# Expert weights loaded in 8 KB runs, with the inner channels reordered as the weights are split on ScalarE and VectorE

## The chip, the cores and the metric

The kernel runs on one core of a Trainium2 chip. The metric is device time in microseconds (us), from the start of the program to its end. Engines are PE (TensorE: matmuls; PEld its weight loads), DVE (VectorE), ACT (ScalarE), POOL (GpSimd) and SP (SyncE, which here only issues DMAs).

## The reference

One layer over 2048 latent tokens of width 1024 with a context prefix of 256: a mixing sub-layer (retention and Mamba-2 heads) and then a mixture of gated-MLP experts. The change is in the second. Each token picks one of 4 groups and two of its 8 experts, and each of the 32 experts works on its tokens in blocks of 128:

```python
def expert_block(args):
    tok, e = args
    xb = h_pad[tok]
    hid = jax.nn.silu(xb @ w_gate[e]) * (xb @ w_up[e])
    return hid @ w_down[e]
```

Per expert, `w_gate` and `w_up` are 1024 x 512 and `w_down` is 512 x 1024, all fp32: 2 MB each. The router's logits are `h @ w_rg` and `h @ w_re`, from the same normed rows `h`.

## The kernel before

The program has five stages: `front`, `states`, `mixing`, then `residual` and `experts` in one program, and `combine`. Every product is made of three: a value is split into a high part (rounded to fp32r) and a low part (the rest), and high x high, high x low and low x high are summed in PSUM.

**residual** goes through 16 tiles of 128 tokens. Per tile it makes the output projection, `x1`, and from it the normed rows `h2`: L2257 scales and L2259 adds, both on DVE, over 128 x 1024. PE transposes `h2` (L2101) in eight chunks of 128 columns, multiplies by the router's weights (L2058), and ACT sends `h2` to `second_norm` in HBM, from which the experts gather their rows. Between L2257 of a tile and its transposes PE works on the products of another tile (L2049). DVE then does the routing (L2186 to L2241). In turns 3 to 8 SP issues the loads of expert 0, and in the last turn ACT makes the high part of its first third (L2138), ahead of its copy L2160.

**experts** holds one expert's weights whole in `raw` (`e_w_whole`), and their parts in `wh` (`e_w_high`) and `wl` (`e_w_low`), each as three thirds of 4096 elements per partition. Third 0 is gate and up for the inner channels 0 to 255, third 1 those for 256 to 511, third 2 is the down weights. SP loads each third as two sixths of 1 MB (`load_sixth`): row `k * 128 + p` of gate or up goes to partition p, 256 elements (1 KB) at a time, and rows of down whole, 4 KB. A third of the next expert is loaded when DVE has made the low part of the one in `raw` (`wls`).

A block of 128 tokens is one turn of `body` on each engine. On PE:

- 24 matmuls for the first 256 inner channels, gate and up side by side in one PSUM bank (L2513 high x high, L2514 high x low, L2517 low x high), which need third 0; then 24 for the other 256, which need third 1;
- transposes of the first half of the hidden values (`turn_h`, L2501) and of the next block's rows (`turn_x`, L2494);
- 24 matmuls for down (L2522), 8 of them ahead of the transposes of the second half of the hidden values.

ACT: Silu of each half of the gate (L2578), copies of the transposed hidden values (L2585) and rows (L2566), half of the output (L2593). DVE: Silu(gate) x up x router's weight (`hid`, L2628), the low parts of the transposed values (L2633, L2612), the other half of the output (L2640).

In the last block of an expert (`following` is the next expert) ACT also makes the next expert's high parts (L2573, two instructions of 128 x 2048 per third) and DVE its low parts (L2619, the same): third 0 between the two halves of Silu and of `hid`, third 1 after the transposed hidden values, third 2 after the output. There are 48 blocks for 32 experts in these inputs, so 31 blocks have such a follower's weights to make; below they are called **splitting blocks**. An expert of several blocks goes through `body` without this work first; one of a single block has only a splitting block, so splitting blocks also come one behind the other.

## Time and profile before

| | |
|---|---|
| median of 3 runs | 2333.85 us (2333.26 to 2334.17) |
| profiled execution | 2337.66 us, its span 2336.0 us |
| PE busy | 2177.8 us, 93% |
| DVE busy | 1400.3 us, 60% |
| ACT busy | 1055.3 us, 45% |
| POOL busy | 643.1 us, 28% |
| DMA | 518.11 MB, mean 222 GB/s |

The shares are means over the five stages. The stage of the experts, which the change concerns most, is from 1386.8 us of the span (first matmul) to 2277 us (end of the last).

### The profile page before, as it was taken

What the parts mean: (1) busy time and instruction counts of PE and PEld (TensorE: products, weight loads), DVE (VectorE), ACT (ScalarE), POOL (GpSimd) and SP (SyncE); (2) the same over time, 40 slices, a digit from 0 to 9 for tenths busy, and PEclk for the clock granted to TensorE, in tenths of its full rate; (3) what the DMA queues carried; (4) which work ended last, traced back from release to release, by engine and by line L of the source; (5) the groups of instructions that cost most, each with busy time, mean ns of one, the idle gap of its engine ahead of it and who ended that gap; (6) DMA issues with size and microseconds to landing.
All of it is one profiled execution on the core that took longest, in us unless ns stands there. A gap on an engine that the chain in (4) does not pass through costs nothing. (4 is left out here: it accounts for less than half of the span.)

```text
span 2336.0 us, 35426 instructions
## 1 busy us (share of the span) xinstructions
PE 2177.8 (93%) x11618; PEld 1836.8 (79%) x11619; DVE 1400.3 (60%) x2033; ACT 1055.3 (45%) x1518; POOL 643.1 (28%) x648
## 2 busy tenths in 40 slices
PE   8999999999999679998999979999999999999990
PEld 5888888899999568887788858778788888887770
DVE  6322222377555578887566665765767675647776
ACT  4422332243223026665333234755666665547763
POOL 0000000000000558887222232221333333323333
PEclk9999999999999889999999989999999999999995
DMA  8632333546551987765554335998988887868997
GB/s 308 237 108 109 127 142 139 187 158 214 175 175 54 333 331 240 233 220 203 160 214 150 118 124 168 344 285 256 338 263 268 270 276 244 252 174 278 350 347 302
DMA packets 297436, 518.11 MB, mean 222 GB/s; under 512 B 33492, under 2 KB 206108, under 8 KB 292584
## 3 DMA queue, kind: packets, MB, share of 16 engines
q1 hardware_dynamic: 271000, 439.52, 55.1%
q0 software_dynamic: 17136, 43.92, 8.4%
q10 hardware_dynamic: 9216, 33.56, 3.5%
q8 instruction: 51, 0.84, 0.2%
q14 instruction: 33, 0.27, 0.0%
HBM read 397.28 MB, written 128.57 MB: 225 GB/s over the span
## 5 line engine op out<-in xcount | busy, mean ns | idle before, releaser
L2619 DVE TENSOR_TENSOR e_w_low<-e_w_whole,e_w_high 128x2048 fp32r<-128x2048 f32 x192 | 431.1, 2287 | 90.6 <-ACT e_w_high L2573 87.1
L2573 ACT ACTIVATE e_w_high<-e_w_whole 128x2048 fp32r<-128x2048 f32 x190 | 353.9, 1914 | 30.2 <-DMA e_w_whole<-in_moe_w_down_dram 18.5
L2513 PE MATMUL r_py<-e_w_high,e_xT 128*128 128x512 f32 x768 | 298.9, 389 | 1.2 <-ACT e_xT L2566 1.2
L2514 PE MATMUL r_py<-e_w_low,e_xT 128*128 128x512 f32 x768 | 298.8, 389 | 0.0
L897 PE MATMUL proj_acc<-w_high,hT_high 128*128 128x512 f32 x672 | 263.9, 393 | 0.3 <-DVE hT_low L1010 0.3
L897 PE MATMUL proj_acc<-w_low,hT_high 128*128 128x512 f32 x672 | 262.0, 390 | 0.0
L897 PE MATMUL proj_acc<-w_high,hT_low 128*128 128x512 f32 x672 | 261.7, 389 | 0.0
L2522 PE MATMUL r_py<-e_w_high,e_hT 128*128 128x512 f32 x768 | 226.7, 407 | 18.0 <-ACT e_hT L2585 17.9
L2517 PE MATMUL r_py<-e_w_high,e_xT 128*128 128x512 f32 x768 | 189.9, 389 | 0.0
L2522 PEld LDWEIGHTS r_py<-e_w_high,e_hT 128*128 128x128 f32 x768 | 138.6, 191 | 45.8 <-ACT e_hT L2585 20.6
L2513 PEld LDWEIGHTS r_py<-e_w_high,e_xT 128*128 128x128 f32 x768 | 144.2, 188 | 31.3 <-issue 1.4
L2517 PEld LDWEIGHTS r_py<-e_w_high,e_xT 128*128 128x128 f32 x768 | 144.2, 188 | 29.9
L2514 PEld LDWEIGHTS r_py<-e_w_low,e_xT 128*128 128x128 f32 x768 | 144.2, 188 | 29.9
L887 PE MATMUL proj_acc<-hT_high,w_high 128*128 128x256 f32 x576 | 164.4, 285 | 0.0
L887 PE MATMUL proj_acc<-hT_low,w_high 128*128 128x256 f32 x576 | 164.1, 285 | 0.0
L887 PE MATMUL proj_acc<-hT_high,w_low 128*128 128x256 f32 x576 | 164.0, 285 | 0.0
L1230 DVE SCALAR_TENSOR_TENSOR conv_out<-ch,cw,conv_out 128x258 f32<-128x258 f32 x288 | 119.4, 480 | 72.3 <-ACT conv_out L805 72.2
L897 PEld LDWEIGHTS proj_acc<-w_high,hT_high 128*128 128x128 f32 x672 | 126.5, 188 | 29.5 <-issue 3.5
L897 PEld LDWEIGHTS proj_acc<-w_high,hT_low 128*128 128x128 f32 x672 | 126.3, 188 | 26.5
L897 PEld LDWEIGHTS proj_acc<-w_low,hT_high 128*128 128x128 f32 x672 | 126.4, 188 | 24.9
L2049 PE MATMUL r_py<-r_w_high,r_yT 128*128 128x512 f32 x512 | 142.1, 394 | 0.0
L2423 POOL COPY e_rows_held<-e_rows_held 128x6 int32<-128x6 int32 x48 | 32.2, 672 | 360.6 <-issue 253.1
(311 smaller groups left out, 4196.2 us busy)
## 6 DMA issues: line engine op xcount, KB each, us to landing
e_w_whole<-in_moe_w_gate_dram SPq DMA_DIRECT2D x64, 1024.0 KB
e_w_whole<-in_moe_w_up_dram SPq DMA_DIRECT2D x64, 1024.0 KB
e_w_whole<-in_moe_w_down_dram SPq DMA_DIRECT2D x64, 1024.0 KB
by_token<-tok SPq DMA_DIRECT2D x32, 512.0 KB, 3.0
w_in_raw<-in_w_mod_dram SPq DMA_DIRECT2D x32, 512.0 KB, 4.4
m_tok<-by_token SPq DMA_DIRECT2D x16, 768.0 KB, 5.5
s_kv<-by_token SPq DMA_DIRECT2D x20, 512.0 KB, 5.9
modulated_high<-hT_high SPq DMA_DIRECT2D x9, 1024.0 KB, 3.9
```

What stands on the lines that cost most here:

```text
L887: m = nc.tensor.matmul(bank[:, b * 2 * P:(b + 1) * 2 * P], a[:, PLACE[c], k, w], h[:, s, k], start=(k == 0 and n == 0), stop=(k == KD - 1 ...
L897: m = nc.tensor.matmul(bank, h[:, s, k, span], (wh if high_ else wl)[:, PLACE[c], k], start=(k == 0 and n == 0), stop=(k == KD - 1 and n = ...
L1230: V.scalar_tensor_tensor(out=v[:, c], in0=chb[:, c, k:k + OUT], scalar=cw[:, k, c:c + 1], in1=v[:, c], op0=ALU.mult, op1=ALU.add).then_inc ...
L2049: m = nc.tensor.matmul(py[:, s, n], yT[:, s, part, k], with_[:, k, n * 512:(n + 1) * 512], start=(k == 0 and part == 0 and with_ is wh), s ...
L2423: nc.gpsimd.tensor_copy(held[:, 0:2], held[:, 1:3]).then_inc(held_on.sem, 1)
L2513: nc.tensor.matmul(pG[:, half], xT[:, 0, k], wh[:, half, w], start=(k == 0), stop=False)
L2514: nc.tensor.matmul(pG[:, half], xT[:, 0, k], wl[:, half, w], start=False, stop=False)
L2517: m = nc.tensor.matmul(pG[:, half], xT[:, 1, k], wh[:, half, k * 512:(k + 1) * 512], start=False, stop=(k == KD - 1))
L2522: m = nc.tensor.matmul(pY[:, n], hT[:, part, k], with_[:, 2, c0:c0 + 512], start=first, stop=last)
L2573: nc.scalar.activation(wh[:, third, part], raw[:, third, part], ACT.Copy).then_inc(whs.sem, 1)
L2619: nc.vector.tensor_tensor(wl[:, third, part], raw[:, third, part], wh[:, third, part].bitcast(F32), ALU.subtract).then_inc(wls.sem, 1)
```

## The change

1. **Loads.** Partition p now takes rows `8p` to `8p + 7` of gate and up. Third 0 holds the first four of these rows with all 512 inner channels of gate and of up, third 1 the other four: one run of 8 KB per partition and sixth. Of down it takes rows `4p` to `4p + 3`, two per sixth, again one run of 8 KB.
2. **Order of the model's channels.** `h2` is written by DVE so that chunk k of its transposes holds channels `8p + k` (`by_chunks`, in L2257 and L2259), and the router's weights are loaded to match.
3. **Order of the inner channels.** Chunk c of the hidden values must hold channels `4q + c`, so gate and up are put in that order as they are split: for thirds 0 and 1 ACT reads `raw` with steps of four elements (16 bytes) and writes runs of 128, and DVE does the same (`sixth_of`). For down both read as before. Gate and up of a chunk lie side by side, and Silu and `hid` read them in runs of 128.
4. **Order of the work.** Third 0 now has half of the rows of all products, so PE makes 24 matmuls with it for both halves of the inner channels, says so (`rows_done`), then 12 with third 1 that end the first half and 12 that end the second. In a splitting block ACT and DVE make the first sixth of the next expert after `rows_done`, ahead of the first Silu and `hid`, and the second sixth behind them.

```diff
@@ residual @@
-                nc.vector.scalar_tensor_tensor(out=h2[:, 1 - s], in0=x1[:, 1 - s], scalar=ss[:, 3:4], in1=g["mod"][:, 2], op0=ALU.mult, op1=ALU.mult).then_inc(h2m.sem, 1)
+                nc.vector.scalar_tensor_tensor(out=by_chunks(h2[:, 1 - s]), in0=by_rows(x1[:, 1 - s]), scalar=ss[:, 3:4], in1=by_rows(g["mod"][:, 2]), op0=ALU.mult, op1=ALU.mult).then_inc(h2m.sem, 1)
...
-                nc.vector.tensor_tensor(h2[:, 1 - s], h2[:, 1 - s], g["mod"][:, 1], ALU.add).then_inc(h2s.sem, 1)
+                nc.vector.tensor_tensor(by_chunks(h2[:, 1 - s]), by_chunks(h2[:, 1 - s]), by_rows(g["mod"][:, 1]), ALU.add).then_inc(h2s.sem, 1)
@@ load_sixth @@
-        to = raw[:, third].rearrange("p (k n f) -> p k n f", k=KD, n=2)[:, :, n]
-        eng.dma_start(to, io[src][0, bass.ds(e, 1), :, third * 256:(third + 1) * 256].rearrange("o (k p) f -> p (o k) f", p=P)).then_inc(landed, 16)
+        rows = KD // 2
+        to = raw[:, third, n * THIRD // 2:(n + 1) * THIRD // 2].rearrange("p (k f) -> p k f", k=rows)
+        eng.dma_start(to, io[src][0, bass.ds(e, 1)].rearrange("o (p k) f -> p (o k) f", k=KD)[:, third * rows:(third + 1) * rows]).then_inc(landed, 16)
...
+def sixth_of(buf, third, n, whole):
+    if third == 2:
+        return buf[:, third, n * THIRD // 2:(n + 1) * THIRD // 2]
+    if whole:
+        return buf[:, third, n * THIRD // 2:(n + 1) * THIRD // 2].rearrange("p (k q c) -> p k c q", q=P, c=DE // P)
+    return buf[:, third].rearrange("p (k c n q) -> p k c n q", c=DE // P, n=2, q=P)[:, :, :, n]
@@ experts, tensor @@
+            pe.wait_ge(xTs.sem, xTs.at(b))
+            pe.wait_ge(wls.sem, wls.at(expert_of[0], 2))
             for half in range(2):
                 pe.wait_ge(hids.sem, hids.at(b - 1, half + 1))
...
+                gate_up(half, 0, 0)
+            pe.wait_ge(xTl.sem, xTl.at(b))
+            for half in range(2):
+                m = gate_up(half, 1, 0)
+            m.then_inc(rows_done.sem, 1)
+            pe.wait_ge(wls.sem, wls.at(expert_of[0], 4))
+            for half in range(2):
+                gate_up(half, 0, 1)
+                gate_up(half, 1, 1).then_inc(prodG.sem, 1)
@@ experts, scalar @@
+        def high_sixth(third, n):
+            nc.scalar.activation(sixth_of(wh, third, n, False), sixth_of(raw, third, n, True), ACT.Copy).then_inc(whs.sem, 1)
...
         def body(b, row, following):
+            if following is not None:
+                act.wait_ge(w_in.sem(0), w_in.at(following))
+                act.wait_ge(rows_done.sem, rows_done.at(b))
+                high_sixth(0, 0)
@@ experts, vector @@
+        def low_sixth(e, third, n):
+            dve.wait_ge(whs.sem, whs.at(e, 2 * third + n + 1))
+            nc.vector.tensor_tensor(sixth_of(wl, third, n, False), sixth_of(raw, third, n, True), sixth_of(wh, third, n, False).bitcast(F32), ALU.subtract).then_inc(wls.sem, 1)
```

How this moves instructions, on ACT, from the start of a splitting block to the copy of the last transposed hidden values. Before (L2578 is Silu into `e_sg`, L2573 makes a high part, L2585 and L2566 are the copies):

```order
L2578 ACT_TABLE_LOAD
L2578 ACTIVATE e_sg<-r_py 128x256
L2570 ISA
L2573 ACTIVATE e_w_high<-e_w_whole 128x2048 x2
L2577 REGISTER_ALU
L2578 ACTIVATE e_sg<-r_py 128x256
...
L2585 ACTIVATE e_hT<-r_pl 128x256
...
L2566 ACTIVATE e_xT<-r_pT 128x1024
L2585 ACTIVATE e_hT<-r_pr 128x256
```

Now the same place of the changed kernel (its L2613 is Silu, L2598 makes a high part, L2619 and L2595 are the copies):

```order
L2598 ACT_TABLE_LOAD
L2598 ACTIVATE e_w_high<-e_w_whole 128x16x128
L2612 ISA
L2613 ACT_TABLE_LOAD
L2613 ACTIVATE e_sg<-r_py 128x256
L2598 ACTIVATE e_w_high<-e_w_whole 128x16x128
L2612 REGISTER_ALU
L2613 ACTIVATE e_sg<-r_py 128x256
L2619 ACTIVATE e_hT<-r_pl 128x256
...
L2595 ACTIVATE e_xT<-r_pT 128x1024
L2619 ACTIVATE e_hT<-r_pr 128x256
```

One conversion stands ahead of the first Silu and one behind it, and there are two loads of an activation table where there was one.

On DVE, the same block from its first `hid` on, before (L2628 makes `hid`, L2619 a low part of the weights):

```order
L2628 SCALAR_TENSOR_TENSOR e_hid<-e_sg,e_rows_held,r_py 128x256
L2618 ISA
L2619 TENSOR_TENSOR e_w_low<-e_w_whole,e_w_high 128x2048
L2618 REGISTER_ALU
L2619 TENSOR_TENSOR e_w_low<-e_w_whole,e_w_high 128x2048
...
L2628 SCALAR_TENSOR_TENSOR e_hid<-e_sg,e_rows_held,r_py 128x256
L2633 TENSOR_TENSOR e_hT<-r_pl,e_hT 128x256
```

and now (L2650 makes a low part, L2666 makes `hid`):

```order
L2650 TENSOR_TENSOR e_w_low<-e_w_whole,e_w_high 128x16x128
...
L2666 SCALAR_TENSOR_TENSOR e_hid<-e_sg,e_rows_held,r_py 128x256
L2649 REGISTER_ALU
L2650 TENSOR_TENSOR e_w_low<-e_w_whole,e_w_high 128x16x128
...
L2666 SCALAR_TENSOR_TENSOR e_hid<-e_sg,e_rows_held,r_py 128x256
L2671 TENSOR_TENSOR e_hT<-r_pl,e_hT 128x256
```

The first low part has moved ahead of the first `hid`; the number of instructions is the same.

## Rows read from the trace of the kernel before

**Rows 1.** Windows: us, busy time (instructions) of each engine, PEclk, DMA share, GB/s.
```profile
1387.00:2277.00 890.00, 862.58 (x4032) 710.94 (x4031) 583.60 (x476) 541.50 (x520) 272.49 (x241) 0.99 0.88 275
1110.00:1340.00 230.00, 224.95 (x1233) 194.07 (x1234) 148.00 (x364) 73.47 (x134) 63.65 (x104) 0.98 0.47 163
2290.00:2336.00 46.00, 0.00 (x0) 0.00 (x0) 37.65 (x32) 18.39 (x32) 17.68 (x16) 0.50 0.92 365
```
**Rows 2.** Timeline of PE, first gate-up matmul of six blocks: start, us, instruction.
```profile
1386.79 0.49 PE L2513 MATMUL r_py<-e_w_high,e_xT 128*128 128x512 f32 x1 [1.19 <-ACT e_xT L2566]
...
1505.91 0.39 PE L2513 MATMUL r_py<-e_w_high,e_xT 128*128 128x512 f32 x1
...
1506.36 0.39 PE L2513 MATMUL r_py<-e_w_high,e_xT 128*128 128x512 f32 x1
...
1526.81 0.39 PE L2513 MATMUL r_py<-e_w_high,e_xT 128*128 128x512 f32 x1
...
1544.52 0.39 PE L2513 MATMUL r_py<-e_w_high,e_xT 128*128 128x512 f32 x1
...
1562.23 0.39 PE L2513 MATMUL r_py<-e_w_high,e_xT 128*128 128x512 f32 x1
...
2259.08 0.39 PE L2513 MATMUL r_py<-e_w_high,e_xT 128*128 128x512 f32 x1
```
**Rows 3.** Groups of instructions, 1340 to 2290: count, busy us, mean ns, idle before.
```profile
L2619 DVE TENSOR_TENSOR e_w_low<-e_w_whole,e_w_high 128x2048 fp32r<-128x2048 f32 x192 | 431.1, 2287 | 90.6 <-ACT e_w_high L2573 87.1 <-issue 3.4
L2573 ACT ACTIVATE e_w_high<-e_w_whole 128x2048 fp32r<-128x2048 f32 x190 | 353.9, 1914 | 30.2 <-DMA e_w_whole<-in_moe_w_down_dram 18.5 <-DMA e_w_whole<-in_moe_w_up_dram 11.7
L2578 ACT ACT_TABLE_LOAD x47 | 60.3, 1283 | 1.1 <-issue 0.3
L2612 DVE TENSOR_TENSOR e_xT<-r_pT,e_xT 128x1024 fp32r<-128x1024 f32 x49 | 59.8, 1220 | 21.6 <-ACT e_xT L2566 21.4
L2566 ACT ACTIVATE e_xT<-r_pT 128x1024 fp32r<-128x1024 f32 x49 | 50.3, 1028 | 25.7 <-PE r_pT L2494 25.7
L2628 DVE SCALAR_TENSOR_TENSOR e_hid<-e_sg,e_rows_held,r_py 128x256 f32<-128x256 f32 x96 | 45.6, 476 | 125.4 <-ACT e_sg L2578 106.9 <-POOL e_rows_held L2423 18.4
L2578 ACT ACTIVATE e_sg<-r_py 128x256 f32<-128x256 f32 x96 | 36.7, 382 | 138.3 <-PE r_py L2517 137.8
L2640 DVE COPY e_y<-r_py 128x512 f32<-128x512 f32 x48 | 32.9, 686 | 65.6 <-DMA rows_summed<-e_y,e_rows_held 42.3 <-PE r_py L2522 23.3
L2593 ACT ACTIVATE e_y<-r_py 128x512 f32<-128x512 f32 x48 | 28.6, 595 | 91.9 <-DMA rows_summed<-e_y,e_rows_held 64.7 <-PE r_py L2522 27.2
L2633 DVE TENSOR_TENSOR e_hT<-r_pr,e_hT 128x256 fp32r<-128x256 f32 x48 | 20.1, 420 | 6.9 <-ACT e_hT L2585 6.9
L2585 ACT ACTIVATE e_hT<-r_pr 128x256 fp32r<-128x256 f32 x48 | 18.5, 386 | 66.0 <-PE r_pr L2501 64.9 <-issue 1.0
```
**Rows 4.** Timeline of DVE in the splitting block that began at 1544.52.
```profile
1556.80 0.48 DVE L2628 SCALAR_TENSOR_TENSOR e_hid<-e_sg,e_rows_held,r_py 128x256 f32<-128x256 f32 x1
```
**Rows 5.** Groups of instructions on DVE, whole span, small and strided ones among them.
```profile
L2206 DVE TENSOR_REDUCE o_s<-o_w 128x8 f32<-128x32 f32 x16 | 3.4, 211 | 0.5
L2235 DVE TENSOR_REDUCE o_sl<-o_wr 128x2 f32<-128x64 f32 x16 | 3.5, 220 | 0.5
L2199 DVE TENSOR_SCALAR o_og<-o_expert_number,o_group_first 128x4 f32<-128x4 f32 x16 | 3.7, 229 | 0.6
L2200 DVE TENSOR_SCALAR o_d<-o_l,o_m 128x4 f32<-128x4 f32 x16 | 3.7, 229 | 0.6
L1812 DVE TENSOR_TENSOR m_t<-m_t 128x512 f32<-128x512 f32 x16 | 20.5, 1279 | 0.0
```
**Rows 6.** DMA queues, 1387 to 2277: packets, MB, share of 16 engines.
```profile
q1 hardware_dynamic: 147718, 202.62, 66.5%
```
**Rows 7.** Timeline of a turn of the residual stage: second step of `h2`, and PE's transposes.
```profile
1300.32 1.23 DVE L2259 TENSOR_TENSOR r_h<-r_h,mod 128x1024 f32<-128x1024 f32 x1
1303.31 1.03 PE L2101 MATMUL r_pT<-ident,r_h 128*128 128x128 f32 x8
```

More of the change, by code:

```diff
@@ L2347, in experts @@
     prodG = kit.counter("e_gate_up", 2, credit=2)
+    rows_done = kit.counter("e_first_rows_used")
     sgs = kit.counter("e_silu", 2, credit=2)
@@ L2504, in body, with gate_up @@
         def body(b, row, following, e=None):
+            def gate_up(half, part, rows):
+                for k in range(4):
+                    w = slice((2 * k + half) * 512, (2 * k + half + 1) * 512)
+                    if part == 0:
+                        nc.tensor.matmul(py[:, 0, half], xT[:, 0, 4 * rows + k], wh[:, rows, w], start=(rows == 0 and k == 0), stop=False)
+                        nc.tensor.matmul(py[:, 0, half], xT[:, 0, 4 * rows + k], wl[:, rows, w], start=False, stop=False)
+                    else:
+                        m = nc.tensor.matmul(py[:, 0, half], xT[:, 1, 4 * rows + k], wh[:, rows, w], start=False, stop=(rows == 1 and k == 3))
+                        if k == 3:
+                            return m
+            pe.wait_ge(xTs.sem, xTs.at(b))
+            pe.wait_ge(wls.sem, wls.at(expert_of[0], 2))
             for half in range(2):
                 pe.wait_ge(hids.sem, hids.at(b - 1, half + 1))
[L2508 to L2518 removed]
+                gate_up(half, 0, 0)
[7 more added lines that the diff above has]
+                gate_up(half, 1, 1).then_inc(prodG.sem, 1)
             def down(k, part, with_, first=False, last=False):
@@ L2571, in high @@
             for n in range(2):
-                part = slice(n * HALF, (n + 1) * HALF)
-                nc.scalar.activation(wh[:, third, part], raw[:, third, part], ACT.Copy).then_inc(whs.sem, 1)
+                high_sixth(third, n)
         def body(b, row, following):
+            if following is not None:
+                act.wait_ge(w_in.sem(0), w_in.at(following))
+                act.wait_ge(rows_done.sem, rows_done.at(b))
+                high_sixth(0, 0)
             for half in range(2):
                 act.wait_ge(prodG.sem, prodG.at(b, half + 1))
-                nc.scalar.activation(sg[:, half], pG[:, half, 0], ACT.Silu).then_inc(sgs.sem, 1)
+                nc.scalar.activation(sg[:, half].rearrange("p (c q) -> p c q", c=2), pG[:, half, :, 0], ACT.Silu).then_inc(sgs.sem, 1)
                 if following is not None and half == 0:
-                    high(following, 0)
+                    high_sixth(0, 1)
             for half in range(2):
@@ L2627, in body @@
                     dve.wait_ge(held_on.sem, held_on.at(b + 2))
-                nc.vector.scalar_tensor_tensor(out=hid[:, half * 256:(half + 1) * 256], in0=sg[:, half], scalar=held[:, 1, 2:3].bitcast(F32), in1=pG[:, half, 1], op0=ALU.mult, op1=ALU.mult).then_inc(hids.sem, 1)
+                nc.vector.scalar_tensor_tensor(out=hid[:, half * 256:(half + 1) * 256].rearrange("p (c q) -> p c q", c=2), in0=sg[:, half].rearrange("p (c q) -> p c q", c=2), scalar=held[:, 1, 2:3].bitcast(F32), in1=pG[:, half, :, 1], op0=ALU.mult, op1=ALU.mult).then_inc(hids.sem, 1)
                 if following is not None and half == 0:
-                    low(following, 0)
+                    low_sixth(following, 0, 1)
             for half in range(2):
```

33 lines of the change are left out of this document (13 added, 20 removed).

## Prediction

> **What bounds the kernel now.** I read the windows by stage first. In the expert stage, 890 us of the span, PE is busy for 862.6 us at a granted clock of 0.99, the upper of its levels (2.4 GHz); DVE is busy for 583.6 and ACT for 541.5, and the DMA engines for 0.88 of the time [rows 1]. So PE sets the end, but nothing is far from full. Then PE's timeline: a block of 128 tokens takes 17.7 us where nothing holds it (1544.52 to 1562.23), with a matmul of 512 columns every 0.226 us, and 20.9 us in others (1505.91 to 1526.81) [rows 2]. From the first block's start to the last one's, 47 blocks, are 872.3 us, 40 more than 47 x 17.71. Counting all starts, ten blocks of 19.9 to 21.7 us hold 31 us of that; they are all splitting blocks that stand behind another splitting block. There are 17 such blocks (I call them **chained**), and 14 splitting blocks stand behind one that does not split. The chained ones take 19.6 us on average. The other excess is mostly the first block's.
>
> What stretches the ten is DMA: ACT sits idle for 30.2 us ahead of its conversions because weights have not landed [rows 3], and what it then makes late delays Silu and PE. That is what longer runs can mend. But the groups also show how little room DVE has. A splitting block holds six low parts of 2.287 us, two `hid` of 0.476, two small low parts of 0.42, one of 1.220 and a copy of 0.686: 17.4 us, in 17.7. ACT has six of 1.914, one table load of 1.283, two Silu of 0.382, two copies of 0.386, one of 1.028 and one of 0.595: 15.9 us [rows 3]. Whatever makes DVE's conversions dearer becomes the period of the chained blocks at once.
>
> **The price of a 16-byte step.** This decides the case. Four of the six conversions now read `raw` so, on both engines. No large instruction here does it; one small one does. L2206 reduces 32 elements that lie 32 bytes apart and takes 211 ns. L2235, the same operation on neighbours, takes 220 ns for 64 [rows 5]. An element costs DVE (2287 - 1220) / 1024 = 1.04 ns [rows 3], so 32 neighbours would take 187. The steps add 24 ns, 0.76 ns an element, and 1.56 us on 2048: a low part of thirds 0 and 1 takes 3.84 us instead of 2.29. Lower bound: no extra, as L2199, with four stepped elements, takes the 229 ns of L2200 with four neighbours (3 ns would be due). Upper bound: 2.5 ns an element, the slowest DVE row (L1812, 512 elements in 1279 ns) [rows 5], 5.1 us. I take the row with the most stepped elements.
>
> The Trainium skill, page "Vector Engine (DVE) Microarchitecture Reference", section "Measured stream behaviour on trn2", says that a port runs at full rate only on runs of at least two adjacent 4-byte words, and gives 1.73 against 1.05 ns per column if one source hops each element. From that page the estimate would be 3.7 us; L2206 agrees.
>
> ACT has no stepped row. Lower bound nothing, 1.91 us; upper bound DVE's whole 3.84. I take the same share of an element as on DVE: 0.76 / 1.04 of ACT's 0.865 ns ((1914 - 1028) / 1024 [rows 3]) is 0.63, so 1.29 us more, 3.20.
>
> **A splitting block behind a block that does not split (14).** From its first matmul: PE has used third 0 after 24 matmuls, at 5.4 us. ACT makes the first sixth until 8.6, loads a table (the second such load in the block, by the order) until 9.9, Silu until 10.3, second sixth until 13.5, second Silu 13.9. DVE makes its sixth from 8.6 to 12.5, `hid` until 12.9, the second sixth from 13.5 to 17.3, second `hid` until 17.8. PE, done with gate and up at 10.9, waits for the first `hid`, works on and waits for the second. That one ends now at 12.8 us (1557.28 [rows 4]), with 5.0 to the next block; 4.0 of these are PE's own work (16 matmuls and two transposes). So the block ends at about 22.0 instead of 17.7: 14 x 4.3 = 60 us.
>
> **The block behind it (14).** ACT's high parts of third 1 are ready at about 21.6 and 24.8, DVE's low parts at 25.4 and 29.3. PE wants them at 22.0 + 5.4 = 27.4 and waits 1.9. DVE's copy and third 2 end at 34.6, 12.6 into this block, and the two `hid` at 13.6, where PE wants the first at 12.8: 0.8. 14 x 2.7 = 38 us.
>
> **A chained splitting block (17).** DVE's own work is 17.4 + 4 x 1.56 = 23.6 us, ACT's 15.9 + 1.3 + 4 x 1.29 = 22.4. Neither fills its time: a low part starts only after its high part, and the first sixth only after PE's 24 matmuls. DVE's idle time before L2619 is now 90.6 us, 2.9 per expert [rows 3]; I leave 1.9. Period 25.5 instead of 19.6: 17 x 5.9 = 100 us. The waits for DMA, some 33 us, are in the 19.6 and so given back here. With this period transfers are hidden: q1 takes 66.5% of 890 us for 202.6 MB, 2.92 us per MB [rows 6], 18 us for an expert's 6.3 MB even at today's price.
>
> **Residual stage.** `h2` is written with 512-byte steps: L2257 costs 0.8 us more for 1024 elements, L2259, which also reads so, 0.8 to 1.6. It ends now 1.8 us ahead of PE's transposes (1301.55 to 1303.31) [rows 7], so a tile adds 0 to 0.6 us; the last tile's, on the way to the routing, adds 1.6 to 2.4 in full. ACT's two early conversions (L2138) stand before the last tile's copy and add up to 2.6, partly at the same time. Together 4 us, between 2 and 14. The router's weight loads and the loads' issues cost nothing: SP is not waited for.
>
> **Sum.** 60 + 38 + 100 + 4 = 202 us. The profiled execution took 2337.7 us (its span 2336.0), 3.8 above the median of the runs: 2337.7 + 202 - 3.8 = 2536 us.
>
> **Rivals.**
> - *The steps are free* (the side of faster). For it: L2199. The Trainium skill speaks for it too: "SBUF — State Buffer", section "Door 1: The DMA port swizzle", has in its note on cachelines that one can "stride for free" over 4 fp32, though it also wants two hits in a 16-byte line, which this step never has; by that rule the time is this rival's. Against it: L2206, where the excess is eight times what L2199 could hide. Then DMA decides: with 4 KB runs the combine stage has 365 GB/s at a DMA share of 0.92 [rows 1], 2.5 us per MB against 2.9. Gate and up, 4.2 MB an expert, save 1.7 us or more of the 3.1 that a long block loses, so some 18 of 33 us come back. Against that stand the table load and the second `hid`, which ends 0.9 us later (13.7 in place of 12.8); 0.3 of that reaches PE in 31 blocks, 9 us. 2337.7 - 9 - 3.8 = 2325 us. It decides if a step costs DVE less than about 0.2 ns, where 17.4 us of work begin to exceed what the block leaves.
> - *Only DVE pays.* ACT has its own access and no row speaks. Then the first low part starts at 7.4 and the second `hid` ends at 16.0: 14 x 2.4 = 34; the block behind 14 x 1.6 = 22; chained blocks at DVE's 23.6 and 0.9 of waits, 17 x 4.9 = 83. With 4: 143 us, 2477. If a step costs DVE half, about 2410.
> - *Steps cost much more*, as L1812's 2.5 ns would have it on DVE with ACT at 3.84. DVE then has 28.7 us in a chained block and a period near 30.7: 17 x 11.1 = 189, the pairs 14 x 10 = 140, residual 14: about 2675. Against: POOL works beside L1812, and L2206 shows half of its excess per element.
> - *The change doesn't do what it says*: excluded by the order, which shows the conversions as 128x16x128.
>
> **Chances.** Both pay as forecast 0.54, only DVE 0.22, free 0.15, much more 0.09. The point is the likeliest, 2536. The range runs from 2400 (only DVE, at half price) to 2640 (ACT at DVE's price gives 50 to 60 us more, and the cheap end of the last case); it leaves out the free case and the far end of the dear one. About 0.2% (5 us) is what a measurement can tell from no change. Faster by more 0.13, within 0.03, slower 0.84.
>
> **What would show it.** In the profile of the changed kernel: L2650 with the form 128x16x128 near 3.8 us on DVE and L2598 near 3.2 on ACT, while 128x2048 stay at 2.29 and 1.91; two table loads per splitting block; PE waiting for `hid` (transposes L2501's successors) and for low parts of third 1; starts of chained blocks 25 to 26 us apart; ACT no longer idle for weights; q1's time per MB lower although nobody gains by it; the DMA share falling with the longer stage. L2257's successor near 2.0 us. I am wrong if the stepped form takes 2.3 us on DVE, and wrong on the path if it takes 3.8 and blocks stay at 18 to 20 us.

## The result and the profile after

The changed kernel takes **2627.33 us** (median of 4 runs, 2624.16 to 2630.29) against 2334.01 us (4 runs, 2333.26 to 2338.47) of the kernel before, run beside it: ratio 1.1243, 95% interval 1.1223 to 1.1263. It is 293 us slower; the forecast was 202 slower. The profiled execution has a span of 2624.5 us.

The windows by stage, changed kernel (us, busy time and instructions of PE, PEld, DVE, ACT, POOL, then the granted clock, DMA share, GB/s):

```profile
1398.00:2570.00 1172.00, 966.63 (x4032) 769.04 (x4032) 779.26 (x477) 823.34 (x553) 368.53 (x242) 0.91 0.63 209
1110.00:1340.00 230.00, 225.52 (x1234) 193.80 (x1235) 170.31 (x365) 73.62 (x134) 71.10 (x104) 0.98 0.47 163
2577.00:2624.00 47.00, 0.00 (x0) 0.00 (x0) 37.65 (x32) 18.39 (x32) 17.55 (x16) 0.50 0.90 358
```

Against [rows 1]: the expert stage, 890 us before, is 1172 long; the combine stage is as it was, and in the residual window PE's work is as it was, DVE is busier by 22 us and POOL by 7. In the expert stage DVE and ACT are busy for 196 and 282 us more. The DMA share falls from 0.88 to 0.63. The granted clock of TensorE falls from 0.99 to 0.91.

The costliest groups in the expert stage, changed kernel (line, engine, operation, out<-in, shapes, count | busy us, mean ns | idle before and what ended it):

```profile
L2650 DVE TENSOR_TENSOR e_w_low<-e_w_whole,e_w_high 128x2048 fp32r<-128x2048 f32 x190 | 628.7, 3333 | 253.0 <-ACT e_w_high L2598 245.5 <-issue 7.4
L2598 ACT ACTIVATE e_w_high<-e_w_whole 128x2048 fp32r<-128x2048 f32 x186 | 594.5, 3234 | 42.0 <-PE r_py L2530 41.8
L2527 PE MATMUL r_py<-e_w_high,e_xT 128*128 128x512 f32 x768 | 320.9, 418 | 87.6 <-DVE e_w_low L2650 86.3 <-ACT e_xT L2595 1.3
...
L2551 PE MATMUL r_py<-e_w_high,e_hT 128*128 128x512 f32 x768 | 245.4, 433 | 3.5 <-ACT e_hT L2619 3.3
```

The first two answer to L2619 and L2573 of [rows 3]. L2527 is one of PE's matmuls for gate and up; the same of the kernel before, from its profile page:

```profile
L2513 PE MATMUL r_py<-e_w_high,e_xT 128*128 128x512 f32 x768 | 298.9, 389 | 1.2 <-ACT e_xT L2566 1.2
```

One mean covers two kinds: a third of the conversions (down's) have no steps. With 2290 and 1916 ns for these (e3 below shows DVE's alone; ACT's 1916 is the mean of e1, which has no steps), the profile page's means over all 192 and 190 (3340 and 3227 ns) give (192 x 3340 - 64 x 2290) / 128 = 3865 ns for a stepped one on DVE and (190 x 3227 - 64 x 1916) / 126 = 3893 on ACT. ACT no longer sits idle for weights ahead of its conversions: nearly all of the idle time there is for PE (L2530).

Who waits, changed kernel, 1390 to 2570 us (engine, line, waited for: us in total, times, longest):

```profile
DVE e_w_low L2650 <- ACT e_w_high L2598: 245.5, 92, 8.5
...
PE r_pl L2519 <- DVE e_hid L2666: 91.3, 32, 5.7
PE r_py L2527 <- DVE e_w_low L2650: 86.3, 31, 2.9
...
ACT e_y L2627 <- DMA rows_summed<-e_y,e_rows_held: 24.7, 5, 5.6
```

PE waits 32 times for the first `hid` and 31 times for a low part of third 1; there are 31 splitting blocks. DVE in turn waits for ACT.

One chained splitting block. PE's timeline of the changed kernel has its start and the next (start, us, instruction), 27.7 us apart:

```profile
2489.22 0.39 PE L2527 MATMUL r_py<-e_w_high,e_xT 128*128 128x512 f32 x1
...
2516.91 0.39 PE L2527 MATMUL r_py<-e_w_high,e_xT 128*128 128x512 f32 x1
```

ACT's timeline in between (in brackets the idle time ahead and what ended it):

```profile
...
2497.70 1.28 ACT L2598 ACT_TABLE_LOAD   x1
2498.99 4.00 ACT L2598 ACTIVATE e_w_high<-e_w_whole 128x2048 fp32r<-128x2048 f32 x1
2503.01 1.28 ACT L2613 ACT_TABLE_LOAD   x1
2504.30 0.39 ACT L2613 ACTIVATE e_sg<-r_py 128x256 f32<-128x256 f32 x1
2504.59 3.87 ACT L2598 ACTIVATE e_w_high<-e_w_whole 128x2048 fp32r<-128x2048 f32 x1
...
2509.61 1.03 ACT L2595 ACTIVATE e_xT<-r_pT 128x1024 fp32r<-128x1024 f32 x1 [0.60 <-PE r_pT L2512]
2513.37 0.39 ACT L2619 ACTIVATE e_hT<-r_pr 128x256 fp32r<-128x256 f32 x1 [2.74 <-PE r_pr L2519]
```

And DVE's:

```profile
2508.49 3.89 DVE L2650 TENSOR_TENSOR e_w_low<-e_w_whole,e_w_high 128x2048 fp32r<-128x2048 f32 x1 [1.26 <-ACT e_w_high L2598]
2512.29 0.48 DVE L2666 SCALAR_TENSOR_TENSOR e_hid<-e_sg,e_rows_held,r_py 128x256 f32<-128x256 f32 x1
```

ACT is idle for 3.3 us of the 27.7 (0.60 + 2.74), and the 2.74 are a loop: the second sixth of its third 0 ends at 2508.5, DVE makes the low part until 2512.4 and `hid` until 2512.8, PE transposes, and only then has ACT the next thing to do. ACT, not DVE, fills the period.

I sort the 47 blocks between the first and the last start by kind, mean length in us, with the experiments' kernels (their edits follow; the starts are read from PE's timelines):

| kernel | chained (17) | splitting behind a non-splitting (14) | behind a splitting (13) | first block | 47 blocks |
|---|---|---|---|---|---|
| before | 19.64 | 17.74 | 17.70 | 24.3 | 872.3 |
| changed | 27.74 | 23.42 | 21.85 | 27.8 | 1146.2 |
| e1 no steps, 8 KB runs | 20.76 | 18.19 | 17.92 | 29.7 | 906.0 |
| e2 only DVE steps | 24.61 | 20.46 | 19.04 | 27.2 | 1014.7 |
| e3 only ACT steps | 27.40 | 23.43 | 18.94 | 29.6 | 1104.7 |
| e4 no steps, 1 KB (down 8 KB) | 20.71 | 17.92 | 17.70 | 24.9 | 893.6 |
| e6 before, with steps | 26.29 | 22.13 | 21.95 | 23.5 | 1101.0 |
| e7 no steps, 2 KB (down 4 KB) | 20.18 | 17.93 | 17.72 | 24.4 | 884.5 |
| e8 no steps, 4 KB | 19.84 | 17.96 | 17.70 | 24.4 | 878.5 |
| e11 no steps, 4 KB (down 8 KB) | 19.85 | 17.95 | 17.70 | 27.6 | 881.9 |
| e9 as e8, one table load | 19.29 | 17.73 | 17.74 | 27.6 | 869.9 |
| e10 8-byte steps, 8 KB | 20.73 | 18.41 | 17.89 | 28.1 | 906.3 |
| e12 ACT hops on its writes | 27.77 | 23.44 | 22.48 | 27.5 | 1155.3 |

The two blocks that neither split nor stand behind a splitting one take 17.7 us in every kernel. Of the 288.5 us by which the span grew, 273.9 lie between the first and the last block start and 11.6 ahead of them (first start at 1398.4 instead of 1386.8 [rows 2]).

### The profile page after: what moved, and what is told of

Same layout as the page of the kernel before. It is cut to its first block and busy times, and to the rows that moved or that the text cites. A ratio compares the mean times of both kernels' runs of the same rounds, so it can differ in the third digit from the quotient of the medians.

```text
span 2624.5 us, 35409 instructions
## 1 busy us (share of the span) xinstructions
PE 2284.4 (87%) x11618; PEld 1896.4 (72%) x11619; DVE 1627.2 (62%) x2033; ACT 1344.4 (51%) x1549; POOL 754.9 (29%) x648
## 5 line engine op out<-in xcount | busy, mean ns | idle before, releaser
L2650 DVE TENSOR_TENSOR e_w_low<-e_w_whole,e_w_high 128x2048 fp32r<-128x2048 f32 x192 | 636.5, 3340 | 253.0 <-ACT e_w_high L2598 245.5
L2598 ACT ACTIVATE e_w_high<-e_w_whole 128x2048 fp32r<-128x2048 f32 x190 | 605.8, 3227 | 42.0 <-PE r_py L2530 41.8
L2527 PE MATMUL r_py<-e_w_high,e_xT 128*128 128x512 f32 x768 | 320.9, 418 | 87.6 <-DVE e_w_low L2650 86.3
L2528 PE MATMUL r_py<-e_w_low,e_xT 128*128 128x512 f32 x768 | 315.8, 411 | 0.0
L2527 PEld LDWEIGHTS r_py<-e_w_high,e_xT 128*128 128x128 f32 x768 | 154.2, 201 | 133.8 <-DVE e_w_low L2650 99.4
L2551 PE MATMUL r_py<-e_w_high,e_hT 128*128 128x512 f32 x768 | 245.4, 433 | 3.5 <-ACT e_hT L2619 3.3
L2530 PE MATMUL r_py<-e_w_high,e_xT 128*128 128x512 f32 x768 | 205.6, 401 | 0.0
L2452 POOL DMA_INDIRECT e_x<-second_norm,e_ids x48 | 112.6, 2346 | 310.4 <-PE r_pT L2512 281.5
L2441 POOL COPY e_rows_held<-e_rows_held 128x6 int32<-128x6 int32 x48 | 74.8, 1558 | 411.0 <-issue 284.5
L2528 PEld LDWEIGHTS r_py<-e_w_low,e_xT 128*128 128x128 f32 x768 | 154.8, 202 | 32.5
L2551 PEld LDWEIGHTS r_py<-e_w_high,e_hT 128*128 128x128 f32 x768 | 149.8, 207 | 36.0 <-ACT e_hT L2619 7.9
L2530 PEld LDWEIGHTS r_py<-e_w_high,e_xT 128*128 128x128 f32 x768 | 150.9, 197 | 33.2
```

The lines of the kernel that those rows point to most:

```text
L2441: nc.gpsimd.tensor_copy(held[:, 0:2], held[:, 1:3]).then_inc(held_on.sem, 1)
L2452: pool.indirect_dma_start(xb[:], None, dram["h2"], bass.IndirectOffsetOnAxis(ap=ids[:, 0:1], axis=0), bounds_check=SEQ - 1, oob_is_err=Fal ...
L2527: nc.tensor.matmul(py[:, 0, half], xT[:, 0, 4 * rows + k], wh[:, rows, w], start=(rows == 0 and k == 0), stop=False)
L2528: nc.tensor.matmul(py[:, 0, half], xT[:, 0, 4 * rows + k], wl[:, rows, w], start=False, stop=False)
L2530: m = nc.tensor.matmul(py[:, 0, half], xT[:, 1, 4 * rows + k], wh[:, rows, w], start=False, stop=(rows == 1 and k == 3))
L2551: m = nc.tensor.matmul(pY[:, n], hT[:, part, k], with_[:, 2, c0:c0 + 512], start=first, stop=last)
```

## The experiments

**e1: no steps, all else as changed.** The conversions read the landed weights as neighbours.

```
-        return ...rearrange("p (k q c) -> p k c q", q=P, c=DE // P)
+        return ...rearrange("p (k c q) -> p k c q", q=P, c=DE // P)
```

> The changed kernel with loads, order of work and table loads as they are, but ACT and DVE read all sixths of the weights contiguously (same shapes; the inner channels of gate and up then do not match those of down, so the output is not the layer's). Theory A (the 16-byte steps are the whole loss): conversions of thirds 0 and 1 at 2.29 us on DVE and 1.91 on ACT, chained splitting blocks 18 to 20 us apart, the time 2315 to 2335 us. Theory B (the new order of work and the second table load stretch the blocks): conversions as short, but splitting blocks stay several us over 17.7, the time above 2400 us. Theory C (PE's granted clock, 0.91 in the stage now, is lost for another reason than waiting): the clock stays near 0.91 and blocks that wait for nothing are longer than 17.7 us.

Measured: 2381.02 us (2372.44 to 2405.18), ratio 1.0217 (1.0152 to 1.0281). So the steps are worth 2627 - 2381 = 246 of the 293 us (240 by the ratios, each against its own runs of the kernel before; the interval of e1 is 15 us to each side), and what is left of the change is no gain but a loss of about 47. That was the first miss: theory A had a kernel as fast as before or faster. Theory B had more than 2400 us and did not come true either, and C is out: the granted clock is back at 0.98 (1390 to 2250 us). The waits of this kernel, 1390 to 2300 us:

```profile
ACT e_y L2627 <- DMA rows_summed<-e_y,e_rows_held: 125.5, 25, 9.3
POOL e_x L2452 <- DMA e_ids<-tokens_sorted: 114.9, 28, 5.3
DVE e_y L2678 <- DMA rows_summed<-e_y,e_rows_held: 89.3, 18, 8.9
...
ACT L2598 <- DMA e_w_whole<-in_moe_w_up_dram: 7.0, 10, 1.5
```

ACT's waits for weights (30.2 us before [rows 3]) have nearly gone, as the longer runs promised. In their place ACT and DVE wait about twice as long as before ([rows 3] had 64.7 and 42.3) for `rows_summed`, POOL's scatter-add of the last block's rows, which must have read `y` before `y` is written again.

**e4: the same with gate and up in the old 1 KB runs** (down stays at 8 KB), to see whether the runs are to blame.

```
-        to = raw[:, third, n * THIRD // 2:(n + 1) * THIRD // 2].rearrange("p (k f) -> p k f", k=rows)
+        to = raw[:, third].rearrange("p (k n f) -> p k n f", k=KD, n=2)[:, :, n]
```

> As e1_no_steps, but gate and up come in by the loads of before (1 KB runs, 1 MB per sixth as well; down stays at 8 KB; output not the layer's). Theory A says that DMA was what stretched the ten long blocks of before, so this run shows what the 8 KB runs are worth by themselves: ACT again idle for some 20 to 30 us ahead of its conversions for data, and the time 10 to 25 us above e1_no_steps. If the runs' length is worth nothing: within 3 us of e1_no_steps.

Measured: 2363.71 us (2358.1 to 2364.34), ratio 1.0105 (1.0085 to 1.0125): 17 us faster than with 8 KB runs (26 by the ratios), where I had expected it 10 to 25 us slower.

```profile
ACT L2597 <- DMA e_w_whole<-in_moe_w_up_dram: 30.9, 17, 3.2
POOL e_x L2451 <- DMA e_ids<-tokens_sorted: 27.6, 9, 4.1
ACT e_y L2626 <- DMA rows_summed<-e_y,e_rows_held: 18.8, 7, 5.5
```

The last two are rows of e1 too, and a quarter and a seventh as long as there. From this came a theory that I had not had: **long runs on SP's queue hold up POOL's small transfers** (the ids, the row gather, the scatter-add).

**e2: only DVE steps.** ScalarE's conversions read neighbours.

```
-nc.scalar.activation(sixth_of(wh, third, n, False), sixth_of(raw, third, n, True), ACT.Copy)
+nc.scalar.activation(sixth_of(wh, third, n, False), sixth_of(raw, third, n, True, False), ACT.Copy)
 # the last argument: "p (k c q) -> p k c q" in place of "p (k q c) -> p k c q"
```

> As the changed kernel, but ACT reads contiguously and only DVE with 16-byte steps (output not the layer's). Theory A with both engines paying: DVE's stepped low parts 3.85 us, ACT's high parts 1.91; chained blocks near 24.5 us, the time 2460 to 2490 us. If instead the chain through ACT is all that counts (DVE has room to catch up): below 2400 us.

Measured: 2490.61 us (2487.3 to 2493.59), ratio 1.065 (1.0632 to 1.0668).

```profile
L2651 DVE TENSOR_TENSOR e_w_low<-e_w_whole,e_w_high x190: 2270/3863/3971, 1384.3 to 2419.3; 128x2048 fp32r<-128x2048 f32 x190
...
L2599 ACT ACTIVATE e_w_high<-e_w_whole x186: 1902/1917/1948, 1445.9 to 2412.8; 128x2048 fp32r<-128x2048 f32 x186
```

(Least, median and largest ns; first and last start.) As expected: DVE's steps cost 110 us over e1.

**e3: only ACT steps.** VectorE's first source reads neighbours.

```
-nc.vector.tensor_tensor(sixth_of(wl, third, n, False), sixth_of(raw, third, n, True), ...
+nc.vector.tensor_tensor(sixth_of(wl, third, n, False), sixth_of(raw, third, n, True, False), ...
```

> As the changed kernel, but DVE reads contiguously and only ACT with 16-byte steps (output not the layer's). ACT's stepped high parts 3.87 us, so ACT's work in a chained block is 15.9 + 1.3 + 4 x 1.96 = 25.0 us, and DVE's stays 17.4. Theory A: chained blocks near 26 us and the time 2500 to 2540 us, more than with DVE alone stepped. If DVE is what bounds the chained blocks: below 2450 us.

Measured: 2572.19 us (2567.84 to 2577.69), ratio 1.0998 (1.0978 to 1.1017): 191 us over e1, more than expected, and much more than DVE's.

```profile
L2599 ACT ACTIVATE e_w_high<-e_w_whole 128x2048 fp32r<-128x2048 f32 x186 | 593.3, 3227 | 38.8 <-PE r_py L2531 38.7
...
L2651 DVE TENSOR_TENSOR e_w_low<-e_w_whole,e_w_high 128x2048 fp32r<-128x2048 f32 x188 | 427.8, 2290 | 380.3 <-ACT e_w_high L2599 380.3
```

With DVE's price taken away its idle time for ACT is 380 us, and chained blocks take 27.40 against 27.74 with both. ACT's steps alone give nearly the whole chained period; the two prices (110 + 191) overlap in the 246.

**e6: the kernel before, with the steps and nothing else of the change.** DVE's low parts are edited in the same way.

```
-   nc.scalar.activation(wh[:, third, part], raw[:, third, part], ACT.Copy)
+   nc.scalar.activation(runs(wh[:, third, part]), (stepped if third < 2 else runs)(raw[:, third, part]), ACT.Copy)
```

> The kernel before, its order of work and its loads, only that the conversions of thirds 0 and 1 on ScalarE and VectorE read the landed weights with 16-byte steps (the rows of the parts are then in another order, so the output is not the layer's). Theory A (the steps alone cost what they cost in the changed kernel, some 246 us, and the new order of work hardly matters): 2560 to 2600. Rival F (the steps cost this much only because the new order puts ScalarE's first stepped sixth ahead of Silu, where before Silu came first): Silu and the first hid are then not late, only the chained blocks are bound by VectorE's 24 us, and the time is 2440 to 2520.

Measured: 2574.8 us (2573.49 to 2578.85), ratio 1.1024 (1.1004 to 1.1044): 238 us for the steps alone in the old order, against 246 in the new. Where Silu stands has next to nothing to do with their price. 

```profile
L2627 DVE TENSOR_TENSOR e_w_low<-e_w_whole,e_w_high 128x2048 fp32r<-128x2048 f32 x188 | 620.9, 3338 | 140.5 <-ACT e_w_high L2581 136.9 <-issue 3.6
L2581 ACT ACTIVATE e_w_high<-e_w_whole 128x2048 fp32r<-128x2048 f32 x186 | 592.3, 3238 | 0.0
```

ACT's conversions have no idle time at all ahead of them here.

**e10: 8-byte steps**, on both engines. Inner channels in pairs instead of fours; down lands in pairs of rows.

```
-        return ...rearrange("p (k q c) -> p k c q", q=P, c=DE // P)
+        return ...rearrange("p (m q c) -> p m c q", q=P, c=2)
```

> The changed kernel with inner channels in pairs instead of fours: the same conversions read with 8-byte steps on both engines, down lands in pairs of adjacent rows (the same 8 KB runs). It computes the layer. Theory S (a step costs the same as soon as no two neighbours are read together): conversions stay at 3.87 us on VectorE and 3.89 on ScalarE, and the time at 2620 to 2635. Rival T (the price grows with the distance, as every word drags a longer piece of the row along): about 3.1 us on VectorE and 2.6 to 2.9 on ScalarE, and 2470 to 2540 us.

Measured: 2379.76 us (2374.04 to 2388.53), ratio 1.0191 (1.0169 to 1.0213). Both theories missed: this is e1's time.

```profile
L2650 DVE TENSOR_TENSOR e_w_low<-e_w_whole,e_w_high x188: 2278/2291/2358, 1389.8 to 2305.8; 128x2048 fp32r<-128x2048 f32 x188
...
L2598 ACT ACTIVATE e_w_high<-e_w_whole x186: 1901/2047/2143, 1440.3 to 2303.5; 128x2048 fp32r<-128x2048 f32 x186
```

(A third of these conversions, down's, have no steps.) On DVE an 8-byte step costs nothing (2291 against 2290 ns), on ACT under 0.25 us for 2048 elements (2143 at most, against 1916), while one of 16 bytes costs 1.58 and 1.98. The price does not begin where neighbours stop being read together; it lies between 8 and 16 bytes.

**e12: ACT reads in order and writes with hops of 1 KB**; DVE as changed.

```
-nc.scalar.activation(sixth_of(wh, third, n, False), sixth_of(raw, third, n, True), ACT.Copy)
+nc.scalar.activation(walked(wh, third, n, False), walked(raw, third, n, True), ACT.Copy)
 # walked: "p k c q -> p k q c" on both sides
```

> The changed kernel in all, only that ScalarE goes through its conversions in the other order: it reads the landed weights word by word as they stand and writes each of four neighbours 1 KB apart; VectorE goes on reading with 16-byte steps. It computes the layer. Theory W (the price is of reading alone; ScalarE's writes have room): ScalarE's conversions back at 1.91 us, the time as with VectorE's steps alone, 2480 to 2500. Rival X (a write that hops costs as much as a read): 3.8 to 4.0 us each and 2615 to 2640. Rival Y (a hop of 1 KB costs less than one of 16 bytes, but not nothing, as the channels of h2 on VectorE suggest with 0.78 ns an element): 2.8 to 3.6 us, 2530 to 2600.

Measured: 2633.31 us (2627.33 to 2633.54), ratio 1.1264 (1.1237 to 1.1291). Rival X holds: a hopping write costs ACT as much as a stepped read.

```profile
L2604 ACT ACTIVATE e_w_high<-e_w_whole 128x2048 fp32r<-128x2048 f32 x186 | 597.3, 3265 | 40.9 <-PE r_py L2536 40.7
```

**e7, e8, e11: the length of the runs, without steps in the conversions.** e7 has chunks of 128 adjacent rows (gate and up 2 KB, down 4 KB, `h2` plain); e8 has 4 KB for all three; e11 is e8 with down at 8 KB.

```
e7: io[src][0, bass.ds(e, 1)].rearrange("o (k p) f -> p (o k) f", p=P)[:, third * rows:(third + 1) * rows]
e8: io[src][0, bass.ds(e, 1)].rearrange("o (h k p j) f -> p h (o k) (j f)", h=2, k=2, j=2)[:, third]
e11: io["moe_w_down"][0, bass.ds(e, 1)].rearrange("o (p k) f -> p (o k) f", k=DE // P)[:, 2 * n:2 * n + 2]
```

> The changed kernel's order of work (rows split into two thirds, first sixth ahead of Silu), but chunks of 128 adjacent rows as before: gate and up land in runs of 2 KB, down in 4 KB, h2 and the conversions step over nothing. It computes the layer. Theory D (long runs on SP's queue make the small transfers of the others wait; 1 KB gave 1.0105 of the time before, 8 KB 1.0217): 1.003 to 1.013 of the time before, 2340 to 2364 us, with ScalarE waiting 15 to 60 us in all for rows_summed ahead of the copy of y. Rival (the 8 KB version was slower for another reason, such as the place where the bytes land): about 1.02, 2380 us.

> The kernel without steps in the conversions, as the first experiment, only that gate, up and down land in runs of 4 KB instead of 8 (the rows that land together are not the ones that h2's order goes with, and the output is not the layer's). Theory D: between the 1 KB and the 8 KB version, 1.012 to 1.020 of the time before, with ScalarE's wait for rows_summed ahead of the copy of y between 30 and 110 us. Rival (nothing to do with the run length): as the 8 KB version, 1.022, with 125 us of that wait.

> The 4 KB version of the kernel without steps, only that down lands in runs of 8 KB (gate and up stay at 4 KB; the parts' rows are then in another order and the output is not the layer's). Theory D1 (the wait for rows_summed grows with the share of bytes that come in long runs, gate and up's 8 KB weigh twice as much as down's): 1.006 to 1.012 of the time before, ScalarE's wait for rows_summed between 50 and 90 us. Rival D2 (only the pieces in flight beside the scatter-add matter, which are those of down and third 1): 1.015 to 1.022, wait near 125 us. Rival D3 (down's runs do not matter): 1.0042, 50 us.

| | ratio (95%) | us | ACT's wait for `rows_summed` | POOL's for the ids | SP's queue, share of 16 engines' 910 us (us per MB) | gather of rows, issue to landing, median us |
|---|---|---|---|---|---|---|
| e4 (1 KB, down 8) | 1.0105 (1.0085 to 1.0125) | 2363.71 | 18.8 | 27.6 | 64.9% (2.93) | 7.2 |
| e7 (2 KB, down 4) | 1.0081 (1.0064 to 1.0099) | 2354.80 | 32.8 | 36.4 | 60.9% (2.74) | 7.3 |
| e8 (4 KB) | 1.0042 (1.0024 to 1.0060) | 2348.36 | 49.7 | 66.2 | 59.3% (2.65) | 7.5 |
| e11 (4 KB, down 8) | 1.0055 (1.0043 to 1.0067) | 2351.03 | 56.5 | 77.3 | 58.7% (2.63) | 7.5 |
| e1 (8 KB) | 1.0217 (1.0152 to 1.0281) | 2381.02 | 125.5 | 114.9 | 57.2% (2.63) | 8.4 |

The rows behind the last four columns for e8:

```profile
POOL e_x L2452 <- DMA e_ids<-tokens_sorted: 66.2, 18, 5.1
ACT e_y L2627 <- DMA rows_summed<-e_y,e_rows_held: 49.7, 15, 6.5
```
```profile
q1 hardware_dynamic: 52896, 203.44, 59.3%
...
e_x<-second_norm,e_ids POOLq DMA_INDIRECT x48, 7.5
```

The gather's in e1:

```profile
e_x<-second_norm,e_ids POOLq DMA_INDIRECT x48, 8.4
```

Two things move against each other. The weights' transfers get cheaper with longer runs up to 4 KB, and no cheaper from 4 to 8 KB in gate and up (2.63 us per MB in e11 and e1). The waits behind the small transfers get longer at every step. Up to 4 KB the first wins; from 4 to 8 KB only the second is left, and it takes some 30 us (2351.03 to 2381.02; 38 by the ratios). The last column asks the small transfers themselves. Up to 4 KB the gather hardly takes longer (7.2 to 7.5 us; the kernel before, with 1 KB, has 7.5 as well), so much of the growth of the waits there need not be slower transfers: an engine that comes earlier waits longer for the same event (e9 below). With 8 KB it takes 8.4 (8.5 in e10, which also has 8 KB runs), and 0.2 of the difference is POOL's own instruction (L2452, at the mean 1.30 us in e1 and 1.14 in e8). The scatter-add has a median of 9.7 us in e4, 9.6 in e8, 10.0 in e11 and 10.1 in e1. So the theory holds for 8 KB and not for the way there. Why the transfers of one queue slow those of the other, no run shows.

e7 has its `h2` without steps and down at 4 KB, so the rows up to 4 KB differ in more than the runs of gate and up; e11 and e1 differ in these alone. Down's runs matter little: e11 lies 0.0013 above e8, their intervals overlap, and far under e1, so D2 is out; its waits are in D1's range and its time between D1's and D3's. e7 came out where theory D had it. e8 is faster than theory D had it, which knew only the losing side.

**e9: 4 KB and one table load**, the version meant to beat both. `h2` is laid out to match pairs of rows, and a Silu of one element stands ahead of the first sixth.

```
             if following is not None:
+                nc.scalar.activation(dry[:], g["eps"][:, 0:1], ACT.Silu).then_inc(dried.sem, 1)
                 act.wait_ge(w_in.sem(0), w_in.at(following))
```

> The changed kernel's order of work without any step in the conversions: gate and up land in runs of 4 KB (pairs of adjacent rows; h2's channels are laid out to match, with 8-byte steps on the read side), down in 4 KB, and ScalarE does a Silu of one element ahead of the first sixth, so that a splitting block needs one table load instead of two. It computes the layer. Theory (the second table load, 1.28 us on the way to the first Silu, is most of what the new order costs): first hid of a splitting block 1.3 us earlier, 1.0042 of the time before (the 4 KB version) falls by 5 to 12 us, to 0.999 to 1.002, 2332 to 2342. Rival (the load stands beside other work and PE waits for the transfers that free y's buffer): as the 4 KB version, 1.003 to 1.005.

Measured: 2339.13 us (2329.09 to 2348.01), ratio 1.0009 (0.9994 to 1.0024), beside 2336.72 for the kernel before. It is as fast as before and 288 us faster than the changed kernel, not faster than both. Against e8, splitting blocks are 0.23 us shorter (14) and chained ones 0.55 (17), 13 us in all, where the removed load was forecast to show; the first block is 3.2 us longer. Not all that e9 gains over e8 is the load's: its `h2` no longer hops in its writes, and its first block starts 6.5 us earlier (1385.7 against 1392.2). The profile also tells how to read a wait:

```profile
POOL e_x L2456 <- DMA e_ids<-tokens_sorted: 83.5, 25, 6.0
ACT e_y L2632 <- DMA rows_summed<-e_y,e_rows_held: 80.7, 24, 7.6
```

They are longer than e8's although the blocks are shorter: ACT comes earlier and waits for the same event. The sum of such a row is no price; the blocks' lengths are.

**e5: the changed kernel with `h2` made without steps.**

```
-nc.vector.scalar_tensor_tensor(out=by_chunks(h2[:, 1 - s]), in0=by_rows(x1[:, 1 - s]), ...
+nc.vector.scalar_tensor_tensor(out=by_rows(h2[:, 1 - s]), in0=by_rows(x1[:, 1 - s]), ...
```

> The changed kernel, only that the two operations that make h2 write and read neighbours again, so h2's channels stand in another order than the router and the experts' rows expect: the output is not the layer's. Theory A (the steps of the conversions and the order of the blocks hold nearly all): h2's two operations go back from 2.07 and 2.01 us to 1.28 and 1.23, and of a tile's 1.6 us nearly all is hidden; the time falls by 2 to 6 us of 2627, and the first block still starts about 8 to 10 us later than before. Rival E (the 11.6 us by which the first block starts later come from h2's steps on the way to the routing): falls by 9 to 12 us.

Measured: 2642.23 us (2637.21 to 2652.49), ratio 1.1322 (1.1293 to 1.1351). It tells nothing of the time of `h2`: the router reads `h2` too, so the tokens went to other experts.

```profile
L2527 PE MATMUL r_py<-e_w_high,e_xT 128*128 128x512 f32 x784 | 324.7, 414 | 87.6 <-DVE e_w_low L2650 86.3
```

There are 784 of these matmuls, 16 for each of 49 blocks; the 48 blocks of the other kernels need 768. An experiment that changes what the routing sees changes the work.

## Why the prediction was right, and where it was off

**What bounds it: right.** The two engines that convert are the bound, and the transfers are hidden.

**DVE's price: right, with some luck.** Forecast 3.84 us for a stepped low part, from two small rows (L2206 against L2235 [rows 5]); measured 3.87. The two rows differed by 24 ns, with steps of 32 bytes where the change has 16, and the other pair (L2199 and L2200) showed nothing. That hops of another length would cost the same was assumed; e10 shows that it does not hold for 8 bytes.

**ACT's price: too low, and this is the step that failed.** I gave ACT "the same share of an element as on DVE", 3.20 us between bounds of 1.91 and 3.84. It is 3.89, just above my upper bound: a step costs ACT 0.96 ns an element, DVE 0.77. The effect runs through all block terms:
- *Splitting block behind a block that does not split:* forecast 22.0. Two stepped conversions of ACT stand in its path to the second `hid`, 2 x 0.69 = 1.4 more, 23.4. Measured 23.42. In the block that starts at 1691.84 the second `hid` ends after 19.2 us (17.8 + 1.4) and PE waits for it:

```profile
1710.59 0.48 DVE L2666 SCALAR_TENSOR_TENSOR e_hid<-e_sg,e_rows_held,r_py 128x256 f32<-128x256 f32 x1
...
1711.20 0.44 PE L2519 MATMUL r_pr<-ident,e_hid 128*128 128x128 f32 x2 [0.87 <-DVE e_hid L2666]
```

  So the forecast's path is the one seen, but it is not the only one of that length. e3 takes a step price of 1.6 us out of it, and its blocks of this kind still take 23.43. There PE never waits for the second `hid`, but 31 times for ACT's copy of the first transposed half, which stands behind the second Silu:

```profile
L2552 PE MATMUL r_py<-e_w_high,e_hT 128*128 128x512 f32 x768 | 263.9, 460 | 45.0 <-ACT e_hT L2620 45.0
...
1692.00:1700.00 8.00, 7.75 (x28) 6.28 (x29) 4.26 (x5) 4.98 (x4) 1.21 (x4) 0.79 0.79 277
```

  In one such block PE has just waited 1.27 and 1.93 us; from 1692 to 1700 the clock is granted at 0.79, after 1.00 in the 8 us before, and the mean matmul of down takes 460 ns over the whole stage (407 before, 433 in the changed kernel). The forecast had a term neither for the copy nor for the clock.
- *The block behind it:* forecast 20.4, measured 21.85.
- *Chained:* forecast 25.5 from DVE's 23.6 plus 1.9 of waits. ACT's work, forecast 22.4, is 22.4 + 4 x 0.69 = 25.2, so ACT takes DVE's place as the bound, and its wait for PE's second transposes adds the rest, to 27.74 (through DVE in the changed kernel; e3, without DVE's steps, still has 27.40).

By these lengths the blocks cost 14 x 5.68 + 13 x 4.15 + 17 x 8.10 = 271 us, with 3.5 of the first block 275, where the three terms of the forecast had 198. So 77 of the 91 us missed lie here, and 8 ahead of the first block.

**The residual stage: unit prices right, the path wrong.** L2264 and L2266 take 2.07 and 2.01 us instead of 1.28 and 1.23 [rows 7]:

```profile
L2264 DVE SCALAR_TENSOR_TENSOR r_h<-r_x,r_ss,mod 128x1024 f32<-128x1024 f32 x16 | 33.1, 2072 | 0.6 <-POOL r_ss L254 0.6
L2266 DVE TENSOR_TENSOR r_h<-r_h,mod 128x1024 f32<-128x1024 f32 x16 | 32.1, 2006 | 0.5
```

PE's 225.5 us in the residual window are as before. The first block starts 11.6 us later, where I had 4 (between 2 and 14). Most of that is on POOL, which the forecast left out. POOL's timeline just ahead of the first block, changed kernel, with DVE's low parts beside it:

```profile
1374.67 7.84 DVE L2650 TENSOR_TENSOR e_w_low<-e_w_whole,e_w_high 128x2048 fp32r<-128x2048 f32 x2
1374.94 4.39 POOL L2012 DMA_INDIRECT tokens_sorted<-o_token,slots  x1 [0.30 <-issue]
...
1383.52 7.41 DVE L2650 TENSOR_TENSOR e_w_low<-e_w_whole,e_w_high 128x2048 fp32r<-128x2048 f32 x2
1383.63 8.19 POOL L2037 DMA_INDIRECT e_x<-second_norm,e_ids  x1 [2.21 <-DMA e_ids<-tokens_sorted]
```

and the same two of the kernel before:

```profile
1372.52 2.85 POOL L2004 DMA_INDIRECT tokens_sorted<-o_token,slots  x1 [0.31 <-issue]
...
1379.84 1.05 POOL L2029 DMA_INDIRECT e_x<-second_norm,e_ids  x1 [2.34 <-DMA e_ids<-tokens_sorted]
```

These two instructions take 1.5 and 7.1 us longer, 8.7 of the 11.6; the last `h2` ends 1.4 later. The gather of the first block's rows (L2037) takes 4.3 to 8.2 us in the five kernels in which DVE's low parts have 16-byte steps (changed, e2, e5, e6, e12) and 1.05 to 1.2 in the nine others, e3 with ACT's steps and e10 with 8-byte steps among them. The lengthening goes with DVE's stepped instructions beside it; no run moves the two apart, so the coincidence is all that shows the cause. That 11.6 lies between 2 and 14 is luck: the terms that I gave this range were other ones.

**The 8 KB runs.** "q1's time per MB lower although nobody gains by it" holds: 46.5% of 1180 us for 203.44 MB, 2.70 us per MB instead of 2.92 [rows 6].

```profile
q1 hardware_dynamic: 29088, 203.44, 46.5%
```

But my free-steps rival gave them 18 us to give back, and e1 shows the other sign: without steps they cost 17 us against 1 KB runs. In the changed kernel this is covered by the longer blocks: its wait for `rows_summed` is 24.7 us against e1's 125.5. That rival's 2325 us is refuted twice over: the steps are not free, and if they were the kernel would take 2381. My reading that missing weights stretch the ten long blocks named only one of their causes: in e9 ACT waits for weights ahead of its conversions for 2.5 us in all, and chained blocks still take 19.29 us, with 80.7 us of waiting for `rows_summed`.

**The rule on free strides.** The trace first: 4-byte words 8 bytes apart cost DVE nothing, 16 bytes apart 69% more; ACT's medians are 2047 and 3846 ns, a third of its conversions unstepped in each. The Trainium skill, "SBUF — State Buffer", section "Door 1: The DMA port swizzle", wants two hits in a 16-byte line and says from this that 4 fp32 can be strided for free. The first half agrees with the trace (an 8-byte step hits a line twice, a 16-byte one once); the conclusion drawn from it doesn't. The page of the Trainium skill that I leaned on for DVE, "Vector Engine (DVE) Microarchitecture Reference", section "Measured stream behaviour on trn2", asks for adjacent words; its 1.73 ns per column is near what 16 bytes cost here (3865 / 2048 = 1.89 for the whole operation), but e10's 8-byte steps, which have no adjacent words, run at full rate.

**The rivals.** *Only DVE pays* is excluded by e2 and e3; its 2477 is near e2's 2491, so the working of DVE's share was sound. *Steps cost much more* had ACT at 3.84 in it, which turned out true, but DVE at 5.1, which did not. The measured time lies inside the range because I had let "ACT at DVE's price gives 50 to 60 us more" set its upper end.

**The clock: not foreseen.** It was granted at 0.91 of its upper level in the stage, 0.99 before [rows 1], and the mean matmul of L2527 took 418 ns instead of 389, in a stage in which PE waits for 31 low parts and 59 times for `hid`. Blocks that wait for nothing still take 17.7 us, and e1, which has the same order of work without the steps, is granted 0.98: the clock falls with the stretched blocks. What it costs in them is not separated.
